# Recurrence of a hybrid encoder step: each row load issued as an 88-row and a 40-row transfer

## The reference

```python
h = rmsnorm(x) * (1 + sc1) + sh1
proj = h @ w_in                                  # 4 HGRN2 heads (128 wide) and 8 RWKV-7 heads (64 wide)
# HGRN2, per token: S_t = diag(f_t) S_{t-1} + k_t v_t^T,  o_t = S_t^T q_t
# RWKV-7, per token: S_t = S_{t-1}(diag(w_t) - kk_t^T (a_t*kk_t)) + v_t^T k_t,  y_t = S_t r_t
x = x + g1 * (concat([norm(o) * silu(gate), groupnorm(y) * g]) @ w_out)
x = x + g2 * hier_moe(rmsnorm(x) * (1 + sc2) + sh2)   # top-1 of 4 groups, top-2 of 8 SwiGLU experts
y = rmsnorm(x)
```

## Time and profile before

| | us |
|---|---|
| median of 3 runs | 3236.12 (3233.19 to 3237.65) |
| profiled execution, its own time | 3231.98 |
| its span, first to last instruction | 3230.2 |
| PE busy | 2943.0 (91%) |
| PE weight loads busy | 1735.1 (54%) |
| DVE busy | 1410.5 (44%) |
| ACT busy | 974.7 (30%) |
| mean granted TensorE clock | 0.956 |
| `recur`, first load issued to last store issued | 1107.4 to 1796 |

### The profile page before, as it was taken

The page is one execution under the profiler, slowest core; times in us unless marked ns, Lnnn a source line. Parts: engine busy times, 40 slices in busy tenths (PEclk is TensorE's granted clock), DMA queues, the critical chain, the costliest instruction groups (busy, mean ns, idle before and its releaser), DMA issues. The chain is left out here.

```text
span 3230.2 us, 68743 instructions
## 1 busy us (share of the span) xinstructions
PE 2943.0 (91%) x28939; PEld 1735.1 (54%) x28940; DVE 1410.5 (44%) x3438; ACT 974.7 (30%) x1872; POOL 162.0 (5%) x248
## 2 busy tenths in 40 slices
PE   6998999999999488888898599949999999999988
PEld 2432455454555378778787355535555555555543
DVE  2245466665655545666666144451221122212217
ACT  2456334343334223333332122102222212222215
POOL 0000000000000000000000000001011001111104
PEclk8999999999999789999999699979999999999998
DMA  7531123242332586555661643465786478767758
GB/s 270 209 130 56 50 93 116 92 138 85 109 132 86 163 220 181 155 153 156 173 181 37 213 162 115 152 170 205 286 323 255 152 262 308 254 230 276 253 196 332
DMA packets 373371, 575.75 MB, mean 178 GB/s; under 512 B 31246, under 2 KB 231110, under 8 KB 370088
## 3 DMA queue, kind: packets, MB, share of 16 engines
q1 hardware_dynamic: 335112, 470.72, 43.2%
q0 software_dynamic: 18080, 72.10, 6.4%
q10 hardware_dynamic: 19968, 29.83, 3.2%
HBM read 427.04 MB, written 145.54 MB: 177 GB/s over the span
## 5 line engine op out<-in xcount | busy, mean ns | idle before, releaser
L451 PE MATMUL pj_P<-pj_hT,pj_wc 128*128 128x448 f32 (+2 forms) x1600 | 592.0, 517 | 0.9 <-ACT pj_stage L579 0.9
L2493 PE MATMUL moe_PG<-wgu,moe_xT 128*64 128x256 f32 x5248 | 582.1, 380 | 0.7 <-ACT moe_xT L2391 0.7
L2493 PEld LDWEIGHTS moe_PG<-wgu,moe_xT 128*64 128x64 f32 x5248 | 377.5, 137 | 226.0 <-issue 47.2
L451 PEld LDWEIGHTS pj_P<-pj_hT,pj_wc 128*128 128x128 f32 x1600 | 294.8, 189 | 257.5 <-issue 241.2
L2500 PE MATMUL moe_PTY<-wd,moe_hT 128*64 128x512 f32 x1312 | 317.7, 603 | 0.0
L2394 ACT ACT_TABLE_LOAD x82 | 105.2, 1283 | 483.1 <-issue 483.0
L1978 PE MATMUL merge_PO<-merge_w,merge_mT 128*128 128x512 f32 x544 | 240.9, 601 | 1.6 <-DMA merge_w<-in_w_out 1.6
L1978 PEld LDWEIGHTS merge_PO<-merge_w,merge_mT 128*128 128x128 f32 x544 | 103.3, 192 | 126.6 <-issue 123.9
L2357 DVE COPY moe_hT<-moe_PH 128x128 f32<-128x128 f32 x164 | 47.8, 292 | 281.0 <-PE moe_PH L2485 281.0
L2353 DVE TENSOR_TENSOR moe_sg<-moe_sg,moe_PG 128x128 f32<-128x128 f32 x164 | 46.4, 283 | 282.7 <-ACT moe_sg L2394 282.7
L2360 DVE COPY moe_y<-moe_PTY 128x512 f32<-128x512 f32 x82 | 56.7, 692 | 208.3 <-PE moe_PTY L2500 208.3
(11 more groups left out here) (385 smaller groups left out, 4140.2 us busy)
## 6 DMA issues: line engine op xcount, KB each, us to landing
wgu<-in_w_gate SPq DMA_DIRECT2D x32, 2048.0 KB, 9.4
wgu<-in_w_up SPq DMA_DIRECT2D x32, 2048.0 KB, 15.0
wd<-in_w_down SPq DMA_DIRECT2D x32, 2048.0 KB, 16.6
re_hkf<-scratch_hk SPq DMA_DIRECT2D x60, 640.0 KB, 8.0
re_rkf<-scratch_rk SPq DMA_DIRECT2D x68, 320.0 KB, 6.6
scratch_hk<-pj_hk SPq DMA_DIRECT2D x16, 1344.0 KB, 5.8
scratch_y_rows<-moe_y ACTq DMA_DIRECT2D x164, 128.0 KB, 5.2
scratch_rk<-pj_rk SPq DMA_DIRECT2D x16, 1120.0 KB, 4.4
```

Of the source, the lines that this page charges most:

```text
L451: ins = eng.matmul(bank[:, 0:wp], wc[:, j, k, :], hT[:, k, k0:k0 + wp], start=(k == 0), stop=(k == KD - 1), skip_group_check=True)
L2493: ins = eng.matmul(PG[64 * c:64 * c + 64, j, 0:256].rearrange("p (a b) -> p a b", a=2), x_rows, wgu[p][:, :, k, o:o + 128], start=(k == 0) ...
```

## The change

Each load that SP issues for a tile goes as two transfers, of rows 0 to 87 and of rows 88 to 127, instead of one of 128 rows. They go over fewer of the transfer engines. The count that each waiting engine expects is doubled. ACT's four loads of `hk` of tile 0 stay whole and add 32 each. Stores, the loads of constants and decode states, and all other functions stay as they were.

```diff
+            def load(out, src, name):
+                for rows_of in (slice(0, 88), slice(88, 128)):
+                    eng.dma_start(out[rows_of], src[rows_of]).then_inc(ev(name), 16)
             def load_rk(f):
                 k, p = 128 * f, f % 2
                 for c in range(4):
-                    eng.dma_start(rkf[p][:, c, :, :], rk3[:, c, :, k:k + 128]).then_inc(ev(f"rk_in{p}"), 16)
+                    load(rkf[p][:, c, :, :], rk3[:, c, :, k:k + 128], f"rk_in{p}")
             def load_hk(f):
-                        eng.dma_start(hkf[p][:, c, :, :], hk3[:, c, :, k:k + 128]).then_inc(ev(f"hk_in{p}"), 16)
+                        load(hkf[p][:, c, :, :], hk3[:, c, :, k:k + 128], f"hk_in{p}")
...
             def load_back(f):
-                    eng.dma_start(arb[p][:, c, :, :], rk3[:, c, RK_A0:RK_A1 + 1, k:k + 128]).then_inc(ev(f"back_in{p}"), 16)
-                eng.dma_start(qbb[p][:, :, :], hk3[:, :, HK_B, k:k + 128]).then_inc(ev(f"back_in{p}"), 16)
-                eng.dma_start(tmb[p][:, :, :].rearrange("p a b -> p (a b)"), t["tm"][k:k + 128, :]).then_inc(ev(f"back_in{p}"), 16)
+                    load(arb[p][:, c, :, :], rk3[:, c, RK_A0:RK_A1 + 1, k:k + 128], f"back_in{p}")
+                load(qbb[p][:, :, :], hk3[:, :, HK_B, k:k + 128], f"back_in{p}")
+                load(tmb[p][:, :, :].rearrange("p a b -> p (a b)"), t["tm"][k:k + 128, :], f"back_in{p}")
...
-                eng.wait_ge(ev(f"back_in{p}"), 96 * (b // 2 + 1))
+                eng.wait_ge(ev(f"back_in{p}"), 192 * (b // 2 + 1))
...
-                    eng.wait_ge(ev(f"hk_in{p}"), 64 * (f // 2 + 1) + (64 if f == TAIL else 0))
+                    eng.wait_ge(ev(f"hk_in{p}"), 128 * (f // 2 + 1) + (128 if f == TAIL else 0))
...
-                eng.wait_ge(ev(f"rk_in{p}"), 64 * (f // 2 + 1))
+                eng.wait_ge(ev(f"rk_in{p}"), 128 * (f // 2 + 1))
...
-                eng.dma_start(hkf[0][:, c, :, :], hk3[:, c, :, 0:128]).then_inc(ev("hk_in0"), 16)
+                eng.dma_start(hkf[0][:, c, :, :], hk3[:, c, :, 0:128]).then_inc(ev("hk_in0"), 32)
```

More of the change, by code:

```diff
@@ L1023, in load_hk @@
                     if f < TAIL:
-                        eng.dma_start(hkf[p][:, c, :, :], hk3[:, c, :, k:k + 128]).then_inc(ev(f"hk_in{p}"), 16)
+                        load(hkf[p][:, c, :, :], hk3[:, c, :, k:k + 128], f"hk_in{p}")
                     else:
                         for s0, s1 in ((0, levels(f)), (N_LEVELS, N_HK)):
-                            eng.dma_start(hkf[p][:, c, s0:s1, :], hk3[:, c, s0:s1, k:k + 128]).then_inc(ev(f"hk_in{p}"), 16)
+                            load(hkf[p][:, c, s0:s1, :], hk3[:, c, s0:s1, k:k + 128], f"hk_in{p}")
             def load_back(f):
@@ L1777, in _ @@
             p = TAIL % 2
-            eng.wait_ge(ev(f"back_in{p}"), 96 * (TAIL // 2 + 1))
+            eng.wait_ge(ev(f"back_in{p}"), 192 * (TAIL // 2 + 1))
             eng.wait_ge(ev("state_in"), 16 * (3 + NSEQ))
```

## The result

| | before | after |
|---|---|---|
| median, us (4 runs each) | 3236.89 (3233.19 to 3237.71) | 3270.45 (3253.96 to 3296.57) |
| ratio | | 1.0123, 95% interval [1.0093, 1.0154] |
| profiled execution, span | 3230.2 | 3252.2 |
| mean clock | 0.956 | 0.955 |

The change makes the kernel slower, by about 1.2%; the ratio comes from all runs, and the two medians alone give 3270.45 / 3236.89 = 1.0104. The profiled execution of after is the fastest of its four; what the slower ones add has no trace.

What follows compares the result with a forecast made beforehand. PE was taken to be bound by instruction packets arriving late while loads run. Holes gone, 51 us, less 5 for the first load gave -46: 3236.1 to 3190 us; forecast's own range 3178 to 3210, wide range to 3295.

Steps and rivals of the forecast that it cites:

- Is the q8 engine free?: In the recurrence, the engine carrying PE's instruction packets is among the five left without loads; chance 0.70.
- The holes: PE's idle time put down to "issue" in the recurrence's tiles goes if q8's engine has no loads; 51 us gained.
- The bound: In the recurrence, PE stands because instruction packets come late while loads run; two costliest "issue" lines 26.1 us together.
- My 3.27 us a tile: Gain for each of 13 recurrence tiles, 37.15 us against 33.88 in the last prompt tile, the control; 42.5 us.
- Longer bursts: A recurrence tile's load burst grows from 20.0 to 29.1 us on the busiest engine, still fitting a 33.9 us tile.
- My upper bound: Split loads go over 8 and 8 engines, 16 rows on each; the burst takes 38.3 us and bounds the tile.
- First load: PE's wait for rk of tile 0, 26.4 us, gets longer by 5 us, at most 6.
- Who needs the loads: Loads in the recurrence still land in time, the tightest with 11 us of cover; cost nothing.
- SP: 14 more load issues per tile, 7 us on top of 18.8, hold up nobody; cost nothing.
- rival B: Transfers bound the recurrence's tile at 36 to 38 us, giving the gain back; -15 to +15 us, chance 0.05.
- Rival A: q8's engine is one with 12 rows, so packets are late for longer in each tile; +66 us, chance 0.22.
- Rival C: PE's holes are not late instruction packets, or halves still use all engines; 0 to +6 us, chance 0.03.

Runs made afterwards that it cites:

- h1: Kernel before, but from tile 2 on each load is one transfer of rows 0 to 87, the other rows left out; 3269.43 us, ratio 1.0098.
- e4: Kernel before, but from tile 2 on every load moves rows 0 to 15 alone, the rest left out; 3176.87 us, ratio 0.982.
- j1: f2, but hk loads read rows 0 to 63, then 64 to 127 of device memory, still writing even, then odd SBUF rows; 3202.84 us.
- j2: f2, but hk loads write SBUF rows 0 to 63, then 64 to 127, still reading even, then odd device memory rows; 3264.43 us.
- e1: Kernel before with each load of a tile as two transfers, rows 0 to 63 and 64 to 127; 3301.36 us, ratio 1.0197.
- f2: Kernel before with each SP load as two transfers, the even rows and then the odd rows; 3204.18 us, ratio 0.9915.
- e2: Kernel before with each load as two transfers, rows 0 to 119 and 120 to 127; 3316.84 us, ratio 1.025.
- g3: Kernel before, but from tile 2 on hk loads move rows 0 to 99, to fill ten engines, other loads rows 0 to 15; 3189.08 us.

## Why the prediction was wrong

**The failed step is "Is the q8 engine free?", and with it the term of *The holes*, -51 us.** I read one missing start in 14 against 15, took the order of starts for the order of engine numbers, and gave the result 0.70. The engine's load was to fall away and the holes with it. In h1, whose loads are one transfer of rows 0 to 87, they did not: tiles of 37.5 us and not 33.4, 61.3 us of "issue" waits where before has 58.0, each hole of 1 us and more still ending 1.3 to 1.6 us behind a q8 packet. Splitting off rows 88 to 127 frees the fetch of nothing: after, the waits rose to 69.3 us. Whether the engine is among the loaded ones, or the fetch suffers in another way, stays open. The order of starts within 0.15 us was no evidence of numbers, and by the count of engines alone the chance was 5 in 16.

**The bound was read rightly.** The holes are late instruction packets, and late by the loads: without most of the load bytes the kernel takes 3177 us, the floor that the forecast's range gave (3178). My 3.27 us a tile were taken between 13 tiles with a mean clock of 0.97 and a control with 1.00, so they held the clock's part too, about 1 us; in e4 it came back with the holes. The packets are late, not slow. Over 6 us of an `hk` burst, one takes 1.2% of 16 x 6 us = 1.15 us before (1495.5 to 1501.5), and 1.4% = 1.3 us after (1476 to 1482):

```profile
q8 instruction: 1, 0.02, 1.2%
```

```profile
q8 instruction: 1, 0.02, 1.4%
```

**Longer bursts: right in kind, for another reason.** I forecast 20 to 29 us, from 12 rows instead of 8 on the busiest engine, at 200 GB/s; it went from 22 to 34. `hk` runs at 154 GB/s. A transfer of 88 rows is slow by itself, 153 GB/s in h1 and not 207; with halves it is the written rows that make it slow (j1, j2), and for 88 rows that is argued, not shown. My upper bound was a worse count of engines; that an engine could be slower with the same rows was in none of my cases, though I had written that the profile has no transfer of that form.

**First load:** +5 forecast, 32.5 - 26.4 = +6.1 measured. It didn't reach the total in this execution: from the end of that wait to the first mark PE took 33.0 us, where before took 37.6, and `project`, which is the same, happened to end 4.9 us earlier. The loss is in the tiles behind the first mark. **Who needs the loads, SP:** as forecast, nobody waits in the loop, and rival B fell with that. With a longer burst the cover was thinner than 11 us, and still enough.

**Rival A came nearest, at half its price.** Its burst was even too short; yet it said +66 and the median is +33.6, the profiled execution +22. Its premise, the q8 engine among those that carry 12 rows, fits h1 and isn't proven. It took 9 us more of burst to cost 3.5 us of each tile. Measured are 12 us more and 37.91 - 37.15 = 0.76 us a tile: a tile loses 37.15 - 33.88 = 3.3 us in a burst of 22 before and 4.0 in one of 34 after, 0.15 and 0.12 us for each us. In e1 it is 7.4 us in a burst of 29, 0.26 for each. So a price for each us of burst, which is how rival A was worked out, is not what the runs show, and none of them shows what to put in its place.

**Rival C,** that the holes aren't late packets, is refuted by e4 and by the packet behind every hole. The page of the Trainium skill that it leaned on, "Runtime: NRT & Kernel Launch", section "Instruction fetch mechanics", calls the fetch mostly hidden. In this kernel it isn't: with the clock that it takes down, it costs 59 us of 3237, and PE stands until 1.2 to 1.7 us after a packet has landed.

## What to carry to other kernels

Write all 128 rows, or rows spread over all of them, in each transfer: 64 neighbouring rows of SBUF move at 203 to 210 GB/s, every other row at 283, whatever rows are read. If a written-out loop has idle time put down to "issue" while loads run, look whether each hole ends a fixed time behind an instruction packet (here 1.2 to 1.7 us); then the packets are late. Cut each load in two over all rows (here 0.9915 [0.9899, 0.9932], the best version), keep the burst dense, and don't count on an engine being free unless a run has shown it. When a run leaves data out, check that the stages behind it still do the same work.

## What the runs showed that I had not expected

- Loading 88 rows alone (h1) saves nothing in the recurrence, 591.5 us from the first tile mark to the last against 582.9, at 153 GB/s. Its time of 3269.43 us also holds two more blocks of `experts`, some 25 us.
- Shorter holes give back clock as well: 0.97 before, 0.99 in f2, 1.00 in e4, worth 1.1 us of the 3.7 us a tile.
- Splitting off only eight rows costs most: e2 is the slowest of all, 1.025 [1.0219, 1.0281], at 190 GB/s.
- Ten engines kept busy cost nothing in the first five tiles of g3 and 2.2 us a tile from then on.
- Twice as many transfers, half as long, gain 0.7 to 0.9%; four times as many gain no more, and half as many cost 0.2% [0.02%, 0.33%].
- Five engines kept full at 20 GB/s each for 13 us of every tile cost nothing (3176.16 against 3176.87 us).
